# Reordered input projections of a gated delta rule and of two mLSTM layers in a one-core kernel

## What is computed

```
def gdn_prep(z, conv_w, a_log, dt_bias, n_seg, seg_len):
    qkv, gate, a_f, a_b, b_f, b_b = split_last(z, (3 * GDN_W, GDN_W, GDN_H, GDN_H, GDN_H, GDN_H))
    qkv = jax.nn.silu(short_conv(qkv, conv_w, n_seg, seg_len)).astype(F32)
    q, k, v = jnp.split(qkv, 3, axis=-1)
    shared = (l2norm(to_heads(q, GDN_H)) * GDN_D ** -0.5, l2norm(to_heads(k, GDN_H)), to_heads(v, GDN_H))
```

## Time and profile before

| what | value |
|---|---|
| runs | 4978.39, 4977.19, 4970.17 us; median 4977.19 |
| profiled execution | 4974.26 us, span of its instructions 4972.5 us |
| TensorE busy | 4254.7 us, 86% of the span |
| VectorE, ScalarE, GpSimd busy | 32%, 18%, 12% |
| mean granted TensorE clock | 0.896 |

### The profile page before, as it was taken

The page is one execution under the profiler, slowest core; times in us unless marked ns, Lnnn a source line. Parts: engine busy times, 40 slices in busy tenths (PEclk is TensorE's granted clock), DMA queues, the critical chain, the costliest instruction groups (busy, mean ns, idle before and its releaser), DMA issues. The chain is left out here.

```text
span 4972.5 us, 53519 instructions
## 1 busy us (share of the span) xinstructions
PE 4254.7 (86%) x22156; PEld 2705.7 (54%) x22156; DVE 1594.6 (32%) x3484; ACT 891.8 (18%) x1726; POOL 615.1 (12%) x666
## 2 busy tenths in 40 slices
PE   6768878798879599999999788778989989669899
PEld 3448778375534554444444347666555547666554
DVE  2662444212323510111111353622144253631251
ACT  4211222112110011000000410111044210110251
POOL 3001332003100211000001300111000100111001
PEclk8888888795588799999999899889999999889999
DMA  5100000205211221111110201211010210011101
GB/s 184 71 5 6 2 2 2 83 30 180 68 65 59 85 101 34 43 34 43 34 42 30 110 26 43 85 49 42 26 39 22 75 68 25 8 57 42 55 12 45
DMA packets 170752, 252.63 MB, mean 51 GB/s; under 512 B 6149, under 2 KB 137393, under 8 KB 169617
## 3 DMA queue, kind: packets, MB, share of 16 engines
q1 hardware_dynamic: 154320, 169.62, 10.7%
q0 software_dynamic: 16192, 79.60, 4.2%
HBM read 214.59 MB, written 34.60 MB: 50 GB/s over the span
## 5 line engine op out<-in xcount | busy, mean ns | idle before, releaser
L710 PE MATMUL ps<-big 128*128 128x512 f32 (+1 forms) x1872 | 711.5, 542 | 46.9 <-ACT big L801 36.8
L732 PE MATMUL ps<-big 128*128 128x256 f32 (+1 forms) x2944 | 578.4, 358 | 40.9 <-DMA big<-hs_scratch 28.3
L710 PEld LDWEIGHTS ps<-big 128*128 128x128 f32 x1872 | 357.8, 192 | 392.9 <-issue 341.2
L732 PEld LDWEIGHTS ps<-big 128*128 128x128 f32 x2944 | 509.4, 194 | 102.5 <-issue 30.7
L2417 PE MATMUL ps<-big 128*128 128x512 f32 x1024 | 442.3, 594 | 8.6 <-issue 8.6
L2431 PE MATMUL ps<-big 128*128 128x512 f32 x1024 | 440.8, 592 | 0.0
L2328 PE MATMUL ps<-big 128*128 128x512 f32 (+1 forms) x896 | 359.3, 562 | 3.0 <-DVE big L3518 2.0
L2481 DVE SCALAR_TENSOR_TENSOR big<-ps,big 128x512 f32<-128x512 f32 x128 | 96.1, 751 | 776.6 <-PE ps L2431 776.6
L2417 PEld LDWEIGHTS ps<-big 128*128 128x128 f32 x1024 | 195.1, 191 | 254.2 <-issue 254.2
L2431 PEld LDWEIGHTS ps<-big 128*128 128x128 f32 x1024 | 194.6, 190 | 244.9 <-issue 244.9
L2328 PEld LDWEIGHTS ps<-big 128*128 128x128 f32 x896 | 169.6, 190 | 187.7 <-issue 180.8
(11 more groups left out here) (463 smaller groups left out, 5526.7 us busy)
## 6 DMA issues: line engine op xcount, KB each, us to landing
big<-in_w_mlp SPq DMA_DIRECT2D x32, 1024.0 KB, 5.4
big<-in_w_in SPq DMA_DIRECT2D x29, 1024.0 KB, 5.3
big<-in_w_mod SPq DMA_DIRECT2D x24, 1024.0 KB, 5.3
big<-in_w_ada SPq DMA_DIRECT2D x24, 1024.0 KB, 5.1
big<-hs_scratch POOLq DMA_DIRECT2D x8, 2048.0 KB, 10.8
hs_scratch<-big POOLq DMA_DIRECT2D x3, 5120.0 KB, 16.0
big<-c_dft SPq DMA_DIRECT2D x12, 1024.0 KB, 5.5
xs_scratch<-big POOLq DMA_DIRECT2D x16, 640.0 KB, 3.3
```

What stands on the lines that cost most here:

```text
L710: t = e.matmul(b[:, 0:n], wv[:, k, 128 * m:128 * m + 128], K.hT[:, k, t0:t0 + n], start=(k == 0), stop=(k == 7))
L732: t = e.matmul(b[:, 0:nn], K.hT[:, k, 128 * i:128 * i + 128], wv[:, k, 0:nn], start=(k == 0), stop=(k == 7))
```

## The change

- Parameters of all gates are loaded once, at the start, by 12 small DMAs on SP's queue ahead of the first weights, into columns of their own.
- DVE zeroes only the padding of the buffers zs (a few columns), ahead of the gates' rows.
- The gates' rows use three banks (4, 5, 6), not two.
- GdnProj: q's tiles leave out the context (two blocks, not three). q has a buffer of its own in token order (qtm). The transposes of every tile stand behind the next tile's matmuls, over the borders of q, k and v too. Gate columns stand behind k's first tile, the squares and scaling of q between DVE's convolutions of later tiles, PE's part of q's normalize within the gate's projection, and k's whole normalize at the end.
- MlProj: DVE and ACT wait at the start only for PE and DVE of the stage before. Of the gates' chain on DVE the first pieces stay ahead and the rest goes one piece behind each of the first five convolutions. The gate columns stand ahead of the last tile's transposes, which move into v's projection. In the second layer q leaves out the context.
- Each eighth of XT is stored under a semaphore of its own, and scratch of the first RMS norm lies elsewhere.

```diff
@@ class Setup
+    def sync(self, e):
+        ...
+        e.wait_ge(*self.at("par zero"))
+        for d in range(2):
+            r = slice(32 * d, 32 * d + 4)
+            e.dma_start(K.gdn_par[r, 0:1], column(A["gdn_dt_bias"][0, d])).then_inc(L.sem, L.up(by=16))
+            e.dma_start(K.gdn_par[r, 1:2], column(A["gdn_a_log"][0, d])).then_inc(L.sem, L.up(by=16))
+        ...
@@ class ConvProj
+    def pads(self, e, V, c):
+        for z in c.zs:
+            lat, end = c.lat(z), c.wl + c.pad + TC
+            e.memset(lat[:, :, 0:c.pad], 0.0).then_inc(V.sem, V.up())
+            e.memset(lat[:, :, c.pad + c.seg:], 0.0).then_inc(V.sem, V.up((self.tag, "pads zero")))
+            ...
@@ class GdnProj, tensor
-        branch("q")
-        e.wait_ge(*self.at("gdn rows"))
-        ...
-        normalize("q", m.vtm)
-        branch("k")
-        normalize("k", m.ktm)
-        branch("v")
-        self.tm(e, P, "gate", 384, range(8), Banks(K, (0, 1, 2, 3)))
+        def after(n):
+            if n:
+                turned(n - 1)
+            if n == 3:
+                gate_columns()
+        def gate(c, t):
+            if (c, t) == (0, 3):
+                turned(8)
+            if (c, t) == (0, 7):
+                normalize("q", m.qtm)
+        for j, what in enumerate("qkv"):
+            self.cm(e, P, what, 3, cm, self.convs[what].blks, lambda i: after(3 * j + i))
+        self.tm(e, P, "gate", 384, range(8), cm, gate)
+        normalize("k", m.ktm)
@@ class GdnProj, scalar
+        for n, (what, i) in enumerate(self.tiles):
+            self.conv_copies(e, S, self.convs[what], i)
+            if n == 4:
+                e.wait_ge(*self.at("gdn kd"))
+        ...
+            if n == 6:
+                factors("q")
+            self.conv_silu(e, S, self.convs[what], i)
+        gates(0)
+        e.wait_ge(*self.at("x away", self.tag))
+        normalize("q", m.qT)
+        gates(256)
+        factors("k")
+        normalize("k", m.kT)
@@ class GdnProj, vector
-        branch("q", m.vtm)
-        ...
-        normalize("q", m.vtm, 96 ** -0.5)
         e.wait_ge(*self.at("x away", self.tag))
-        branch("k", m.ktm)
-        normalize("k", m.ktm, 1.0)
-        branch("v", m.vtm)
+        for n, (what, i) in enumerate(self.tiles):
+            if n:
+                turned(n - 1)
+            self.conv_vector(e, V, self.convs[what], i)
+            if n == 3:
+                gate_columns()
+            if n in (4, 5):
+                squares("q", range(4 * n - 16, 4 * n - 12), n == 5)
+            if n in (6, 7):
+                scaled("q", range(4 * n - 24, 4 * n - 20), 96 ** -0.5)
+        turned(8)
+        squares("k", range(10), True)
+        scaled("k", range(10), 1.0)
@@ class MlProj, tensor
-        self.cm(e, P, "qk", 8, Banks(K, (0, 1, 2, 3)), then=lambda i: turned(i - 1) if i else None)
-        turned(7)
+        for j in (0, 4):
+            self.cm(e, P, "qk", 4, cm, self.convs[j].blks, lambda i: turned(i - 1), j)
+        gate_columns()
+        self.tm(e, P, "v", 512, range(10), cm, lambda c, t: turned(7) if (c, t) == (0, 4) else None)
@@ class MlProj, vector
-        self.begin(e)
+        self.begin(e, "tensor", "vector")
+        self.pads(e, V, self.convs[4])
+        self.rows_out(e, V, m.G)
+        gates = self.gates(e, V)
+        next(gates)
+        next(gates)
         ...
         for i in range(8):
             if i:
                 turned(i - 1)
-            self.conv_vector(e, V, self.conv, i)
-        turned(7)
+            self.conv_vector(e, V, self.convs[i], i)
+            next(gates, None)
```

More of the change, by code:

```diff
@@ L695, in fresh, with cm @@
         K.hT, K.hx, K.made = K.hT0, "", (tag, set())
-    def cm(self, e, P, what, ntile, ring, blks=BLKS, then=None):
+    def cm(self, e, P, what, ntile, ring, blks=BLKS, then=None, j0=0):
         K = self.K
-        for j in range(0, ntile, 2):
-            nt = min(2, ntile - j)
+        for j in range(j0, j0 + ntile, 2):
+            nt = min(2, j0 + ntile - j)
             used, wv = K.W.use(e, 128 * nt)
@@ L880, in wcol, with parts @@
                 return K.vec[gw][:, c:c + 1]
-            return Conv(what, 3, 7, 64, wcol, None, m.zs, lambda i: m.conv, True)
+            return Conv(what, 3, 7, 64, wcol, None, m.zs, lambda i: m.conv, True, BLKS[0:2] if what == "q" else BLKS)
         self.convs = {"q": conv("q", 0), "k": conv("k", 3), "v": conv("v", 6)}
+        self.tiles = [(what, i) for what in "qkv" for i in range(3)]
+        self.tm_of = {"q": m.qtm, "k": m.ktm, "v": m.vtm}
+    def parts(self, what):
+        return [(0, 4), (4, 4)] if what == "q" else [(0, 4), (4, 4), (8, 2)]
     def sync(self, e):
@@ L1035, in normalize, with squares @@
+        def squares(what, tiles, last):
+            tm, ss = self.tm_of[what], m.ss[what]
+            for t in tiles:
+                e.wait_ge(V.sem, V.n)
                 e.tensor_tensor(m.nt, tm[:, t, :], tm[:, t, :], ALU.mult).then_inc(V.sem, V.up())
                 e.wait_ge(V.sem, V.n)
-                e.tensor_reduce(m.ss[:, t, :], h4(m.nt, 96), AXX, ALU.add).then_inc(V.sem, V.up())
+                e.tensor_reduce(ss[:, t, :], h4(m.nt, 96), AXX, ALU.add).then_inc(V.sem, V.up())
+            if last:
+                x = ss[:, 0:tm.shape[1], :]
@@ L1044, in normalize @@
-            for t in range(10):
+            if scale != 1.0 and tiles[0] == 0:
+                x = ss[:, 0:tm.shape[1], :]
+                e.tensor_scalar(x, x, scale, None, ALU.mult).then_inc(V.sem, V.up())
+            e.wait_ge(V.sem, V.n)
+            for t in tiles:
                 x = h4(tm[:, t, :], 96)
-                e.tensor_tensor(x, x, bc(m.ss[:, t, :], 96), ALU.mult).then_inc(
+                e.tensor_tensor(x, x, bc(ss[:, t, :], 96), ALU.mult).then_inc(
                     V.sem, V.up((self.tag, what, "scaled", t)))
-        branch("q", m.vtm)
@@ L2755, in vector @@
                 chained(e.memset(MP[q, 9:10], NEG))
+        yield
         H = slice(0, 64)
@@ L2785, in turned, with values @@
                     V.sem, V.up(("free", u, 0)))
+        def values(c0, tiles):
+            for t in tiles:
+                u = (tag, "v", c0, t)
+                e.wait_ge(*self.at("mm", u))
+                e.tensor_copy(m.v5[:, t, c0 // 128:c0 // 128 + 2, 0:128],
+                              self.bank(u)[:, 0:256].rearrange("p (h x) -> p h x", h=2)).then_inc(
+                    V.sem, V.up(("free", u, 0)))
         for i in range(8):
```

296 lines of the change are left out of this document (151 added, 145 removed).

## The result

| what | before | after |
|---|---|---|
| time, median (range) | 4977.04 us (4970.17 to 4978.39) | 4825.5 us (4822.87 to 4827.15) |
| span of the profiled execution | 4972.5 us | 4823.7 us |
| TensorE busy | 4254.7 us | 4229.0 us |
| mean granted TensorE clock | 0.896 | 0.902 |

The change makes the kernel faster: ratio 0.9698, 95% interval 0.9681 to 0.9715. The forecast was 4816 us with a range of 4794 to 4846, so the time lies 9.5 us above the forecast and inside the range.

The account below looks back on a forecast made before the run. TensorE was taken as the bound, standing still in three projections. Gains of 77.6, 46.0 and 38.1 us less 1 at the start made 160.7, so span 4811.8, time 4813.6, and 4816 us on the runs' scale; range 4794 to 4846.

Parts of the forecast that it names:

- The bound and the scheme: Three projections: TensorE sets the pace once its waits go, 17.2 us a tile, 13.75 without the context.
- The rival of another engine: Delta-rule and mLSTM tiles: DVE or ACT sets the pace, 2 us lost per tile, 30 us, 4846; chance 0.13.
- The new bank waits: Gate columns: the fifth needs a bank DVE frees behind a convolution; some 12 us in delta rule, about 8.5 per mLSTM.
- The rival without them: Gate columns of all three projections: no bank waits, 29 us less, 4787 us; chance 0.06.
- The restart: Behind the delta rule's column wait: 3 us for remaining columns and ends at low clock, 0.9 for a slow restart.
- The end of the delta rule: Delta rule's projection: the stage ends at 337.3 us, 77.6 us gained.
- The start: Ahead of the first weights: 12 parameter loads on SP delay by 0 to 6.6 us, taken as 1 us.
- First and second mLSTM: mLSTM projections: 46.0 us gained in the first, 38.1 in the second, 13.8 of the latter from q's context.
- The reading of the earlier trace: First mLSTM projection before: PE's 18.23 us wait for ACT's copies comes from gates' chain and zeroing on DVE.
- The rule against it: First mLSTM: GpSimd's rescaling of XT and two-input DVE instructions lock each other out; 8.7 us, 3 on the sum.
- The low clock: About 650 us of matmuls in the three projections run at half clock, 5466 us; chance 0.02.

Follow-up runs that it names:

- the first mend: Changed kernel with DVE's copies of the gate columns ahead of a convolution, not behind it (mLSTM: behind the seventh tile): 4782.06 us, ratio 0.9616.
- The doubled loads: Changed kernel with the 12 parameter loads issued twice on SP, the second set into spare columns: 4825.5 us, ratio 0.97.
- both mends: Changed kernel with DVE's gate-column copies ahead of a convolution and ACT's factors for k ahead of its half-width gate-tile copies: 4778.63 us, ratio 0.9609.

## Why the prediction was right, point by point

- **The bound and the scheme held.** PE waited where the rows said, and with the waits gone its own work sets the pace: 17.2 us a tile, 13.75 without the context, gate 13.8 and half-width tiles 14.3, all as counted. The rival of another engine falls: with four squares DVE had 0.72 us of idle time before the next tile's copies, where the count had 0.7.
- **The new bank waits were foreseen and real.** 10.98 us against "some 12", and the fifth mLSTM column started 10.3 us behind the last tile against 10.4. The rival without them is what the first mend makes; its 29 us were too few, as the mend gave 41: it had priced the waits alone.
- **The restart was mis-sized.** This is the term that failed. The sum had 3 us for the columns and ends and 0.9 for k's second tile; they took 4.6 and 19.77 - 17.2 = 2.6. In the mLSTM stages the sum had 4.4 us for columns and ends, which took 5.9, and nothing for v's first five tiles, which took 20.14 and 18.77 us against 17.28. That is 3.3 us in the delta rule, where 2.2 are missing, and 4.4 and 3.0 us in the mLSTM stages, where 4.0 and 2.6 are missing; the rest was made up by small gains (in the delta rule the wait in the columns was about 1 us shorter than counted, and q's normalize 0.5).
- **The end of the delta rule** was forecast at 337.3 and came at 338.4, the 4 us wait in front of k's normalize included. That it is so near is in part luck: counted from q's first tile it came 2.3 us late, and the start was 1.2 us early where 1 us late was forecast.
- **The start** was forecast to lose 1 us and gained 1.2. The doubled loads show that SP's issues cost nothing. What gave the 1.2 us was not tried apart; q's first tile started between 107.4 and 109.0 us in the profiled runs, which all have this part of the change, so much of it is scatter.
- **First and second mLSTM:** 46.0 forecast, 42.0 measured; 38.1 forecast, 35.5 measured. The reading of the earlier trace rows named the chain and the zeroing together. Taken apart, in the changed kernel the chain alone is worth 7.6 us in the first stage and nothing in the second, the padding behind it another 10.6 and 6.2.
- **The rule against it** holds, in another form than I gave it. I bounded it at 8.7 us on DVE, for instructions with two inputs. Measured were 6.7 us on three instructions with one input, and 0.7 on L2802, which has two (2.21 us against 1.48). The Trainium skill ("SBUF — State Buffer", "Who interferes with whom") names copies and tensor_scalar as able to contend with GpSimd; the trace agrees with that. In the changed kernel PE has no wait there, so it fell into the slack.
- **The low clock** as a rival of 650 us was far off: in these stages the clock is 1.00 except behind the waits (0.50, then 0.88 and 0.92 in v's first tiles, and 0.76 in k's normalize). But lower clocks are a good part of why the span misses by 11.9 us, in small pieces: 10.7 us behind the waits in the columns, and 2.9 us in the scan of the delta rule, where a turn at 0.76 instead of 0.82 shows it. For the 3.0 us between the mLSTM projections no stretch was taken apart, and the cause stays open. Against these 16.6 us stand 4.7 us of gains that the sum didn't have, 2.2 of them at the start.

## What to carry to other kernels

A wait on TensorE can cost its own length and slow work behind it: three waits of together 26 us were worth 41 here. When matmuls are reordered, write down for each bank who frees it and what stands ahead of that copy in its engine's queue; a copy of 0.2 us behind a convolution of 11 us was the whole wait here. Gains of a few us in a kernel of this length are to be read stage by stage in the profile, and with care even there, since stages without any edit moved by 3 us either way and one by 5.5.

## What the runs showed of the hardware

- DVE instructions with one input from SBUF (COPY and TENSOR_SCALAR, f32) took longer beside GpSimd's tensor_tensor: 2.46, 3.37 and 3.37 us instead of 0.89, 0.82 and 0.82. Each ended some 0.7 us behind the end of a pair of GpSimd instructions. The instruction that starts at 2743.28 ends at 2746.65, 0.69 us behind the end of a pair of GpSimd instructions that began 0.19 us after it and ran back to back until 2745.96. DVE copies out of PSUM in the same stretch kept their 0.69 and 0.42 us, and POOL's pair its 2.5.
- The granted clock fell to 0.50 behind waits of 10.98 and 7.57 us and came back to 1.00 during the next tile; once, in both mends, a tile had 0.91 where PE had waited only 0.27 us ahead of it.
- 45 and 90 additional transposes ahead of a scan with many short waits did not lengthen the whole kernel measurably (ratios 0.9696 and 0.9701 against 0.9698, each within about 0.0014), though they are 5 and 10 us of PE's time.
